# Compressed attention's out-projection in three products of rounded halves, with GpSimd making the rests

## What is computed

```python
proj = h @ w_in                      # queries, 6 key/value parts, gates
k_cmp = compress_blocks(k_c, ...)    # silu(z @ w1) @ w2
o_cmp, o_sel, o_win = ...            # three attentions over compressed, selected, windowed keys
o = gts[:, :, 0] * o_cmp + gts[:, :, 1] * o_sel + gts[:, :, 2] * o_win
return o.reshape(B, S, Q_WIDTH) @ w_o          # out-projection, 1024 x 1024
```

## Time and profile before

| | |
|---|---|
| median of 3 runs | 2094.74 us (2094.38 to 2099.61) |
| profiled execution | 2096.68 us, its span 2094.8 us |
| TensorE (matmul) busy | 2041.1 us, 97% |
| VectorE busy | 875.6 us, 42% |
| ScalarE busy | 696.4 us, 33% |
| GpSimd busy | 29.2 us, 1% |
| mean granted TensorE clock | 0.993 |
| stage `nsa` to the end of its out-projection | 1725 to 1897.6 us of the span |

### The profile page before, as it was taken

One profiled execution on the slowest core, in us unless ns is written; L12 is line 12 of the kernel. 1 busy time (PEld: TensorE's weight loads), 2 busy tenths in 40 slices (PEclk: granted clock), 3 DMA queues, 4 the chain that ended last, 5 costly groups with the idle time before them and its releaser, 6 DMA issues.

```text
span 2094.8 us, 29208 instructions
## 1 busy us (share of the span) xinstructions
PE 2041.1 (97%) x12364; PEld 1440.5 (69%) x12364; DVE 875.6 (42%) x1252; ACT 696.4 (33%) x980; POOL 29.2 (1%) x36
## 2 busy tenths in 40 slices
PE   8999999999999999999999999999999999999998
PEld 7854444434488444444445999899989997758998
DVE  5831111111177111111114656655575568455555
ACT  5521111111254111111113433533353346454333
POOL 1000000000000000000000001000000000000000
PEclk9999999999999999999999999999999999999999
DMA  8689999999947899999999651755266245604620
GB/s 292 239 365 429 428 426 428 429 428 428 411 153 304 367 427 428 428 429 428 428 427 406 227 201 66 280 188 201 102 250 225 97 144 171 242 1 163 239 100 20
DMA packets 117643, 599.25 MB, mean 286 GB/s; under 512 B 6460, under 2 KB 22076, under 8 KB 92973
## 3 DMA queue, kind: packets, MB, share of 16 engines
q1 hardware_dynamic: 115186, 592.01, 70.4%
q0 software_dynamic: 1952, 5.78, 0.8%
q10 hardware_dynamic: 410, 0.09, 0.0%
HBM read 596.81 MB, written 1.05 MB: 285 GB/s over the span
## 4 chain that ended last, share of the span: by engine, by line
PE 81%; DMA 12%; DVE 6%; ACT 1%; issue 1%; ACTq 0%; SPq 0%; DVEq 0%
PE PS L1222 22%; PE PS L1048 15%; PE PS L1236 9%; PE PS L1061 9%; DMA ring<-in_w_expert_up 7%; PE PS L1035 5%; DMA work<-in_w_expert_up 4%; PE PS L894 3%; PE PS L1071 2%; PE PS L946 2%; PE PS L1361 2%; PE PS L1248 2%; PE PS L1553 1%; PE PS L1179 1%; DVE ring_r L2180 1%; DMA ring<-in_nsa_cmp_wv 1%
## 5 line engine op out<-in xcount | busy, mean ns | idle before, releaser
L1585 ACT ACTIVATE split<-ring 128x2048 fp32r<-128x2048 f32 x132 | 253.1, 1920 | 402.6 <-PE PS L1222 268.8
L1048 PE MATMUL PS<-ring,xs 128*64 128x512 f32 x1216 | 367.1, 597 | 9.8 <-DMA ring<-in_w_expert_up 7.0
L2138 DVE TENSOR_TENSOR split<-ring,split 128x2048 fp32r<-128x2048 f32 x132 | 304.1, 2304 | 167.9 <-ACT split L1585 163.1
L1222 PE MATMUL PS<-hT_high,split 128*128 128x256 f32 x2560 | 329.2, 281 | 0.4 <-DVE split L2138 0.4
L1222 PEld LDWEIGHTS PS<-hT_high,split 128*128 128x128 f32 x2560 | 316.5, 189 | 3.4 <-DVE split L2138 0.6
L1048 PE MATMUL PS<-work,xs 128*64 128x512 f32 x832 | 285.1, 604 | 5.9 <-DMA work<-in_w_expert_up 4.1
L1048 PEld LDWEIGHTS PS<-ring,xs 128*64 128x64 f32 x1216 | 117.9, 138 | 185.3 <-issue 185.3
L1236 PE MATMUL PS<-split,ffn_hid 128*128 128x512 f32 x864 | 202.6, 390 | 0.0
L2401 DVE TENSOR_TENSOR work<-PS,work 128x512 f32<-128x512 f32 x32 | 22.1, 692 | 389.8 <-PE PS L1048 389.8
L1236 PEld LDWEIGHTS PS<-split,ffn_hid 128*128 128x128 f32 x864 | 159.7, 188 | 31.7
L1222 PE MATMUL PS<-hT_low,split 128*128 128x256 f32 x1280 | 178.3, 282 | 0.0
(11 more groups left out here) (331 smaller groups left out, 2130.3 us busy)
## 6 DMA issues: line engine op xcount, KB each, us to landing
ring<-in_w_expert_gate SPq DMA_DIRECT2D x38, 2048.0 KB, 26.3
ring<-in_w_expert_up SPq DMA_DIRECT2D x38, 2048.0 KB, 25.7
ring<-in_w_expert_down SPq DMA_DIRECT2D x36, 2048.0 KB, 27.4
work<-in_w_expert_down SPq DMA_DIRECT2D x28, 2048.0 KB, 27.3
work<-in_w_expert_gate SPq DMA_DIRECT2D x26, 2048.0 KB, 29.1
work<-in_w_expert_up SPq DMA_DIRECT2D x26, 2048.0 KB, 23.4
ring<-in_ffn_w_gate SPq DMA_DIRECT2D x20, 2048.0 KB, 8.6
ring<-in_ffn_w_up SPq DMA_DIRECT2D x20, 2048.0 KB, 8.6
```

The lines of the kernel that those rows point to most:

```text
L1048: last = pe.matmul(PS[e * CAP:(e + 1) * CAP, bank, :], xs[:, k, e * CAP:(e + 1) * CAP], slot_of(slots[e], KT)[:, k, :], start=(k == 0), st ...
L1222: last = pe.matmul(PS[:, bank, ft * SEQ:(ft + 1) * SEQ], split_cols(b, kind, part)[:, k, ft * P:(ft + 1) * P], hx[:, k, :], start=(n_ == 0 ...
L1585: return act.activation(o, i, ACT.Copy)
L2138: v.tensor_tensor(at[:, 1], src, at[:, 0], ALU.subtract).then_inc(S.w_low, 1)
```

## The change

1. The out-projection's weights are split: ScalarE copies each half slot rounded into the slot two further on (`wo_split`, slots 2 and 3), and GpSimd subtracts (`ring_r[raw] = ring - high`, four instructions of 128 x 2048). `wo_split(0)` stands before `take_keys(1, 4)` of the first tile, `wo_split(1)` between the two tiles.
2. The outputs are split: `take_outputs` writes `hT_high` and then a float32 copy to one of two rooms `NB.oT`; GpSimd subtracts into `mix_low` (eight instructions of 128 x 256).
3. TensorE makes 3 x 8 products for each tile and column half.
4. `LOADS["nsa"]` is 2, and four slots stay taken until the out-projection is done.
5. `post` of this stage uses `NB.qn` in place of `hp`, which holds `mix_low`. Two semaphores are shared under new names (`yc_gain` becomes `high_made`, `wr_scaled` becomes part of `scaled`), with their counts adjusted.

The pieces of the diff stand in the order table, views, SyncE, GpSimd, TensorE, ScalarE:

```diff
-LOADS = {"mix": 0, "moe": 0, "fin": 0, "ffn": 18, "poo": 2, "nsa": 0}
+LOADS = {"mix": 0, "moe": 0, "fin": 0, "ffn": 18, "poo": 2, "nsa": 2}
...
+        def wo_half(r, half):
+            cols = slice(half * HALF, (half + 1) * HALF)
+            return ring[:, r, cols], ring_r[:, r + 2, cols], ring_r[:, r, cols]
...
                 sp.wait_ge(S.projected, w.to(S.projected, 5))
+                n[0] += 2
                 free[0] = (S.f_done, 2 * TT, None)
-                free[1] = (S.f_done, 0, None)
+                for r in range(1, 4):
+                    free[r] = (S.f_done, 0, None)
...
+            for r in range(2):
+                for half in range(2):
+                    raw, high, low_ = wo_half(r, half)
+                    pool.wait_ge(S.high_made, MIX_HIGHS + 2 * r + half + 1)
+                    pool.tensor_tensor(low_, raw, high, ALU.subtract).then_inc(S.rest_made, 1)
+            for i in range(4 * TT):
+                t, g = i // 4, i % 4
+                pool.wait_ge(S.oT_taken, MIX_UNITS + i + 1)
+                at = (slice(None), slice(2 * g, 2 * g + 2), slice(t * P, (t + 1) * P))
+                pool.tensor_tensor(mix_low[at], NB.oT[i % 2], hT_high[at], ALU.subtract).then_inc(S.rest_made, 1)
...
+                pe.wait_ge(S.rest_made, w.to(S.rest_made, 4))
...
                 for t in range(TT):
+                    pe.wait_ge(S.rest_made, w.to(S.rest_made, 4))
                     for h in range(2):
-                        for m in range(8):
-                            last = pe.matmul(PS[:, 2 * t + h, :], hT[:, m, t * P:(t + 1) * P],
-                                             wv[m // 4][:, m % 4, h * 512:(h + 1) * 512], start=(m == 0), stop=(m == 7))
+                        for n_, (oT, wv) in enumerate(((hT_high, wo[0]), (hT_high, wo[1]), (mix_low, wo[0]))):
+                            for m in range(8):
+                                last = pe.matmul(PS[:, 2 * t + h, :], oT[:, m, t * P:(t + 1) * P],
+                                                 wv[m][:, h * 512:(h + 1) * 512],
+                                                 start=(n_ == 0 and m == 0), stop=(n_ == 2 and m == 7))
                         last.then_inc(S.f_done, 1)
...
-                take_keys(1, 4)
+
+                def wo_split(r):
+                    act.wait_ge(S.loaded[r], w.to(S.loaded[r], 16))
+                    for half in range(2):
+                        raw, high_, _ = wo_half(r, half)
+                        copy(high_, raw).then_inc(S.high_made, 1)
+                    w.past(S.rest_made, 2)
+
+                wo_split(0)
+                take_keys(1, 4, (0,))
+                wo_split(1)
+                take_keys(1, 4, (1,))
...
+                    copy(hT_high[:, 2 * g:2 * g + 2, t * P:(t + 1) * P], o)
+                    if i >= 2:
+                        act.wait_ge(S.rest_made, w.to(S.rest_made))
+                    copy(NB.oT[i % 2], o).then_inc(S.oT_taken, 1)
```

More of the change, by code:

```diff
@@ L41 @@
 STAGES = ["mix0", "moe0", "mix1", "moe1", "final", "ffn00", "pool", "ffn01", "ffn10", "nsa", "ffn11"]
[L43 removed]
+MIX_UNITS = 8
+MIX_HIGHS = 4
+LOADS = {"mix": 0, "moe": 0, "fin": 0, "ffn": 18, "poo": 2, "nsa": 2}
 CONSTS = {}
@@ L443, in nsa_views @@
             b.Sc = [c(16, NCMP) for _ in range(2)]
+            b.oT = [c(2, P) for _ in range(2)]
             c.at = top
@@ L1547, in nsa @@
                 w.past(S.exped, 2)
-                wv = [view(loaded(r), 4, D) for r in range(2)]
+                for r in range(2):
+                    loaded(r)
+                n[0] += 2
                 pe.wait_ge(S.oT_taken, w.to(S.oT_taken, 2))
+                pe.wait_ge(S.rest_made, w.to(S.rest_made, 4))
+                wo = [[ring_r[:, m // 4 + 2 * part, :].rearrange("p (k n) -> p k n", k=4)[:, m % 4, :] for m in range(8)]
+                      for part in (1, 0)]
                 for t in range(TT):
+                    pe.wait_ge(S.rest_made, w.to(S.rest_made, 4))
                     for h in range(2):
-                        for m in range(8):
-                            last = pe.matmul(PS[:, 2 * t + h, :], hT[:, m, t * P:(t + 1) * P],
-                                             wv[m // 4][:, m % 4, h * 512:(h + 1) * 512], start=(m == 0), stop=(m == 7))
+                        for n_, (oT, wv) in enumerate(((hT_high, wo[0]), (hT_high, wo[1]), (mix_low, wo[0]))):
[3 more added lines that the diff above has]
+                                                 start=(n_ == 0 and m == 0), stop=(n_ == 2 and m == 7))
                         last.then_inc(S.f_done, 1)
@@ L1747, in conv_gain @@
                         last = act.activation(yg_high[:, c, :], MB.yc[:, c, :], ACT.Copy, scale=gcT[:, l, c:c + 1])
-                    last.then_inc(S.yc_gain, 1)
+                    last.then_inc(S.high_made, 1)
                 exps(0)
@@ L1953, in take_queries, with take_keys @@
                             .then_inc(S.act_took, 1)
-                def take_keys(br, bank):
-                    for t in range(TT):
+                def take_keys(br, bank, tiles=range(TT)):
+                    for t in tiles:
                         act.wait_ge(S.projected, w.to(S.projected))
@@ L1984, in nsa @@
                 nsa_high(4)
-                for r in (0, 1, 0, 1):
+                for r in range(2):
                     w.past(S.loaded[r], 16)
@@ L2017, in take_outputs @@
                     act.wait_ge(S.oT_done, w.to(S.oT_done))
-                    copy(hT[:, 2 * g:2 * g + 2, t * P:(t + 1) * P],
-                         PS[:, 6 + (t * 4 + g) % 2, 0:SEQ].rearrange("p (s q) -> p s q", s=2)).then_inc(S.oT_taken, 1)
+                    i = t * 4 + g
+                    o = PS[:, 6 + i % 2, 0:SEQ].rearrange("p (s q) -> p s q", s=2)
+                    copy(hT_high[:, 2 * g:2 * g + 2, t * P:(t + 1) * P], o)
+                    if i >= 2:
+                        act.wait_ge(S.rest_made, w.to(S.rest_made))
+                    copy(NB.oT[i % 2], o).then_inc(S.oT_taken, 1)
                 exps(0)
@@ L2106, in take_hT, with add_normed, post @@
                 w.past(S.hT_odd, 2)
-            def add_normed(t):
+            def add_normed(t, room=hp):
                 v.wait_ge(S.root_ready, w.to(S.root_ready))
                 reciprocal(f_rstd[:, t:t + 1], f_root[:, t:t + 1])
-                v.scalar_tensor_tensor(x[:, t, :], hp[:, t, :], f_rstd[:, t:t + 1], x[:, t, :],
+                v.scalar_tensor_tensor(x[:, t, :], room[:, t, :], f_rstd[:, t:t + 1], x[:, t, :],
                                        ALU.mult, ALU.add).then_inc(S.x_ready, 1)
                 v.wait_ge(S.x_ready, w.to(S.x_ready))
-            def post(half=None, between=None):
+            def post(half=None, between=None, room=hp):
                 gain = gain_rows()
```

27 lines of the change are left out of this document (14 added, 13 removed).

## The result

| | before | changed |
|---|---|---|
| median (20 runs each) | 2094.27 us (2090.44 to 2099.61) | 2098.06 us (2094.88 to 2102.55) |
| span of the profiled execution | 2094.8 us | 2096.5 us |

The ratio is 1.0017, with a 95% interval of 1.0009 to 1.0025: 1.9 to 5.2 us slower. That is a slowdown, and one inside the bound of 0.3%. The prediction was 2100.0 us, within 2089.0 to 2105.0.

The account below looks back on a forecast made before the run. TensorE was taken to bound the out-projection, VectorE the stretch just before the attention. Terms -5.8 + 0 + 8.7 + 0.4 + 2.0 = +5.3 us on the median 2094.74 gave 2100.0 us, range 2089.0 to 2105.0.

Parts of the forecast that it names:

- The products: Out-projection on TensorE: 96 fp32r products at the down product's price replace 64 records in 27.72 us; -5.8 us.
- ScalarE's rounding: Before the attention: four weight copies of 1.90 us fit ScalarE's idle time ahead of the keys; 0 us, margins 1.6 and 2.2.
- GpSimd's rests: Before the attention: four weight subtractions of 4.8 us hold VectorE's rotation by turns, delaying its first maximum; +8.7 us.
- The outputs: Attention outputs: ScalarE copies each twice, costing 0.3 on the last and 0.1 on the others; GpSimd's small rests 0; +0.4 us.
- The clock: TensorE's gap before the attention drops it to 1.2 GHz for 5 us, so second-tile scores reach VectorE late; +2.0 us.
- The ring: Start of `ffn11`: down weights requested behind the out-projection still land before ScalarE wants them; 0 us, margin 8.
- a clock that stays low into the units: Rival: TensorE at 1.2 GHz into the attention's units; +6.7 instead of 2.0, 2104.7 us, deciding from 3.0 lost; chance 0.20.
- a clock that stays high: Rival: no clock fall after TensorE's gap, scores and transposes in time; +3.3, 2098.0 us; chance 0.13.
- a VectorE that is not held: Rival: GpSimd's weight subtractions do not hold VectorE's short rotation instructions; -5.4, 2089.3 us; chance 0.10.

Follow-up runs that it names:

- e1: Changed kernel without GpSimd's four weight subtractions, high halves multiplied a second time instead; 2088.87 us beside 2095.86 before, ratio 0.9963.
- e2: Changed kernel with GpSimd making only the first slot's weight rests, second slot's high half multiplied instead; 2090.32 us beside 2095.86 before, ratio 0.9972.
- e9: Changed kernel with 28 unused identity products in TensorE's gap and 6 behind the compressed branch's first turn; 2096.30 us beside 2093.85 before, ratio 1.0013.
- e11: The changed kernel run again, nothing altered; 2098.70 us beside 2094.25 before, ratio 1.0014.
- e4: Kernel before with only the ring shift: next loads two slots on, four slots held until the out-projection ends; 2093.89 us beside 2095.86, ratio 0.9992.
- e7: Changed kernel with each of GpSimd's four weight subtractions cut into four of 512 columns; 2095.58 us beside 2093.85 before, ratio 1.0005.
- e6: Changed kernel with the weights' rests on VectorE, both second-half rests between the two tiles' rotations; 2091.90 us beside 2093.85 before, ratio 0.9988.
- e13: Second run of the changed kernel without GpSimd's weight subtractions, high halves multiplied twice; 2088.92 us beside 2094.25 before, ratio 0.9970.
- e3: Changed kernel with 28 unused identity products in TensorE's gap, behind the first tile's block scores; 2097.33 us beside 2095.86 before, ratio 1.0009.

## Why the prediction was right

- **The products.** Said -5.8; measured 22.05 - 27.72 = -5.67. The down product's price was the right row.
- **ScalarE's rounding.** Said 0, with margins 1.6 and 2.2; idle time left 0.75 and 2.40. In the trace the last projection came earlier than in the kernel before, and the first margin was half used up. e1 has the copies and P to M of 2.10: nothing was lost.
- **GpSimd's rests.** Said +8.7; measured 10.02 - 2.10 = +7.9 in one trace, 8.58 - 2.10 = +6.5 in the other. The mechanism, its turns and the three stretched instructions were as told. The size was 0.8 to 2.2 too large. From GpSimd's start to its end the forecast had 19.7 us (four times 4.8, and VectorE's turns between them); it was 18.15 and 18.19. Of these 1.5 us, 1.0 is the price: 4.54 us each, where the row of 1024 columns, doubled, gave 4.8, perhaps because it counts two starts. The rest is VectorE's turns, which added nothing to GpSimd's time: in e2 two subtractions without a turn of VectorE between them took 9.18, no less than half of the 18.15. The start moved the sum either way: the forecast had it 10.5 us ahead of P, the traces 9.5 and 11.0, which made the delay 1.0 longer in the one and 0.5 shorter in the other; that the first trace comes within 0.8 of the forecast is in part such a cancelling. The Trainium skill (GPSIMD Engine Reference, section 3.1) has 4.5 us for such an instruction of 2048 columns; the trace agrees with its 4.54.
- **The outputs.** Said +0.4; e1 against before, M to O: 59.74 - 59.31 = +0.43. GpSimd's eight small rests cost nothing there: in e1's and the changed kernel's traces VectorE has nothing but reductions of PSUM beside them, and beside one of them its product of 1.23 us, which was not stretched.
- **The clock.** Said +2.0; 61.71 - 59.74 = 1.97 between the changed kernel and e1, and 1.9 against e9. In e11 it was 2.6. The place was as told: the second tile's scores reach VectorE 5.33 us behind the first maximum (5.5 in the forecast, 3.35 before), and the 2.0 us lost there are all that this trace loses up to the out-projection. The length of the fall was mis-sized: it was to last 5 us behind the first maximum, and the clock came back nearly 10 us behind it, in e11 nearly 12. That the further 5 to 7 us cost nothing in the one trace and 0.6 in the other was not forecast; in that the 2.0 owes something to luck.
- **The ring.** Said 0: e4 shows it.
- **Sum.** Said +5.3; the traces give +4.7 and +3.8, the runs +3.8 (1.9 to 5.2). The mis-sized term is GpSimd's rests.
- **The rivals.** The one of a clock that stays low into the units came in its condition and not in its cost: the units' first scores, from 1821 on, ran at the lower clock, which was at 1.00 again from 1826 on (1828 in e11), and 2.0 to 2.6 us were lost of the 3.0 it needed. The one of a clock that stays high is excluded by the row of 1812, the one of a VectorE that is not held by its rows.

## What to carry to other kernels

GpSimd is not free beside VectorE: a subtraction there that reads SBUF held each VectorE instruction with two SBUF operands for up to its whole length (4.5 us for 2048 columns, 1.3 for 512), and the turn came back to GpSimd after one. What it costs is read from VectorE's place in the chain during GpSimd's time, not from GpSimd's idle share: the half of the rests that ended before the critical rotation was free, the other half cost 6.5 to 8 us and, by the gap it made, 2 to 2.6 more of TensorE's clock. Before work is given to the idle engine, look at whether the busy-looking one has waits of the right size at the right place; here VectorE had waits of 4.6, 3.7 and 4.1 us for four subtractions of 2.3, and the same algorithm with the rests there is some 3 to 6 us faster than the kernel before instead of 4 slower.

## What was not expected

- The turns hold between neighbours of one program too: VectorE has L2203 ready directly behind L2202, and GpSimd's next instruction, for which all is ready too, goes first all the same (e7: eight VectorE instructions in a row, each behind one of GpSimd's).
- A held instruction is reported as busy: VectorE's busy time on the page rose by 12.3 us without one instruction more. The mean duration of a group is where to look.
- TensorE's clock fell in the attention in two executions (e6, e13) of kernels without the long gap, at 1.3 to 1.4 us each. It did not in e1, which is e13's code; e6's code has one trace only, and nothing here shows what decides it. With dummies in the long gap it fell behind the next waits (e3). How often it happens was not counted.
- The landing-driven start of the weights' work and the clock of the gates' products move against each other, so that the same delay reads 10.0 in one execution and 8.6 in another. One trace gives a term of 8 us to about 1.5.
